# Giving the low halves of the keys all 128 partitions, so that both score products of a decoder's attention contract over 128 rows

## The chip, the cores and the metric

One Trainium2 chip, one core. The metric is the device time of one execution in microseconds (us), as the median of several runs of the whole kernel; the kernel before takes 1324.79 us (three runs, 1317.44 to 1329.73). Engines are called PE (TensorE), DVE (VectorE), ACT (ScalarE), POOL (GpSimd) and SP (SyncE, which issues most transfers); PEld is the weight-load side of PE.

## What is computed

One inference step of a two-layer trunk for a prompt of 1024 tokens and for 8 samples of 4 new tokens each, all in float32. Layer 0 mixes sparse attention with chunked gating, layer 1 is a gated linear recurrence. The change touches the prompt's attention alone: 8 query heads in 2 groups (one per key/value head of 64 features), three branches merged by gates. Cut to what matters:

```python
qg  = q.reshape(B, T, 2, 4, 64)
s_c = einsum('btghd,bngd->bghtn', qg, kc) * scale + bias      # 16 compressed blocks
s_s = einsum('btghd,bgtkcd->bghtkc', qg, k_s) * scale + b_s   # selected blocks
s_w = einsum('btghd,bkgd->bghtk', qg, kw) * scale + bias      # window of 512
p_x = softmax(where(ok, s_x, NEG))
o   = g0 * p_c @ vc + g1 * p_s @ v_s + g2 * p_w @ vw
```

With 1024 tokens there are 16 blocks and 16 are selected, so the selected branch is plain causal attention over all keys so far.

## The kernel before, in words

The program is written engine by engine, with semaphores. Its stages are: normalising and projecting x (0 to about 394 us in the profile), the prompt's attention, the samples' attention, the output projection of layer 0, the recurrent layer, its output projection.

**Two halves for precision.** PE multiplies a reduced float32 (fp32r) at full speed. So operands are split into a high half, the value rounded to fp32r, and a low half, the rest. `q_hl` holds a tile of 128 queries: for the heads of group g the 64 partitions of that group hold the high half and the other 64 partitions hold the low half. `k_hi` holds the high half of the keys of branch b and group g on both halves of the partitions. So one product over 128 rows gives q_hi k_hi + q_lo k_hi. `k_lo` holds the low half of the keys, of group 0 on partitions 0 to 63 and of group 1 on partitions 64 to 127, so a second product over 64 rows adds q_hi k_lo in the same PSUM bank:

```python
mm(o, q_hl[:, i % 2, h, :], k_hi[:, b, g, keys], True, False)
m = mm(o, q_hl[gp, i % 2, h, :], k_lo[gp, b, keys], False, True)
```

These are lines 1353 and 1354; `mm` is a helper, so the profile gives all its products line 1198, and all transposes line 1202. In both, q is the stationary operand (128 columns) and the keys are streamed, up to 512 columns a product. The probabilities are split in the same way for the product with the values, whose two products over 128 rows (lines 1380 and 1381) also accumulate in one bank.

**Order of the attention.** The prompt has 8 tiles i of 128 queries. A tile has one compressed unit ("c") and 16 units of one head each: for each group g, four heads of the selected branch ("s", (i + 1) * 128 key columns) and four of the window ("w", at most 640 columns). A table written by `attention_steps` (lines 130 to 186) gives the order, the same for PE and DVE and nearly the same for ACT. For each block of 128 keys of a group: PE turns four heads' probabilities (4 transposes, line 1368) into one of three PSUM banks; ACT copies their high half into `p_hl` (line 1056) and DVE subtracts for the low half (line 1837); PE multiplies with the values up to two blocks later. In between PE makes the score products of the next group's heads, one unit per block or more, into one of two slots of two banks; DVE adds the bias and takes the minimum (line 1814; the window's farthest block has a table and a minimum of its own, lines 1808 and 1810), and ACT takes the exponential (line 1048). PE's scores of unit n wait until DVE has read unit n - 2. At the end of a tile's group 16 products bring the outputs back (line 1388), and DVE merges them with the gates (lines 1843 to 1856).

**What runs ahead of it.** When the projections end, ACT copies the high halves (lines 1013, 1017, 1020), POOL copies the windowed keys' high half to the other partitions (line 919) and then clears `aS` (line 923), which the recurrent layer needs; POOL's next work is the second norm's scales (line 826). DVE subtracts for `k_lo` (line 1733) and for the values' low half (line 1738), then waits for the bias, which SP loads in 16 transfers after the last projection (line 696). ACT splits the first queries' high half (line 1036) once the semaphore `split_lo` counts 4; DVE makes their low half (line 1770), and PE begins.

The small buffers `region_m` (spatial weights and their bias, later `aS`, `bS` and `small_out`) and `region_g` (the gating norm's scale and shift, later the final norm's) are not in use during the attention.

Of the kernel before, what the change touches and what calls it, by code (L numbers as in the profile page):

```python
# [23 lines left out]
P = 128  # L24
D = 1024
KC = D // P
SEQ = 1024
# [203 lines left out]
def build(nc, ins, outs):  # L231
    ctx = ExitStack()
    with ctx:
        def sb(name, shape):
            return ctx.enter_context(nc.sbuf_tensor(name, shape, F32))
# [11 lines left out]
        def placed(name, at, shape, dt):  # L247

            return nc.alloc_sbuf_tensor_at(name, shape, dt, offset=arena_at + 4 * at)
# [50 lines left out]
        k_hi = placed("k_hi", AT_W + 8448, [P, 2, KVH, SEQ], F32R)  # L300
        k_lo = placed("k_lo", AT_W + 25600, [P, 2, SEQ], F32R)
        v_hl = placed("v_hl", AT_W + 21504, [P, 2, KVH, PT, 2 * HD], F32R)
# [72 lines left out]
        rel_in = sb("rel_in", [BUCKETS + 1, HEADS])  # L375
        vecT = sb("vecT", [P, NVEC])
        region_m = sb("region_m", [P, 1024])
        wspT = view(region_m, 0, 4, P)
# [429 lines left out]
        def _(pool):  # L808
# [112 lines left out]
            pool.wait_ge(k_hi_other, 2)  # L921
            pool.wait_ge(mix_used, TILES)
            pool.memset(aS, 0.0).then_inc(aS_zero, 1)
            for i in range(TILES):
# [16 lines left out]
        def _(act):  # L941
# [82 lines left out]
            for what, n in act_order(steps):  # L1024
                if what == "split_q":
# [3 lines left out]
                    if n == 0:  # L1029
                        act.wait_ge(fm_dve, counts["dve"])  # L1030
                        act.wait_ge(split_hi, 6)
                        act.wait_ge(split_lo, 4)
                        act.wait_ge(vn_out, 16)
# [162 lines left out]
        def _(pe):  # L1196
            def mm(out, l, r, start, stop):
                return nc.tensor.matmul(out, l, r, start=start, stop=stop, skip_group_check=True)  # L1198
# [124 lines left out]

            pe.wait_ge(split_lo, 4)
            pe.wait_ge(split_hi, 6)
# [5 lines left out]
            for what, n in steps:  # L1331
# [3 lines left out]
                if what == "scores":  # L1335
# [5 lines left out]
                    if kind == "c":  # L1341
                        pe.wait_ge(q_lo, i + 1)
                        for c in range(HPG):
                            m = mm(ps[:, slot, c * 2 * NB:(c + 1) * 2 * NB], qT[:, c, tok(i)],
                                   kc_bd[:, :, :].rearrange("p g n -> p (g n)"), True, True)
                    else:
                        g, b = h // HPG, 0 if kind == "s" else 1
                        gp = slice(g * HD, (g + 1) * HD)
                        for a in range(0, cols, 512):
                            w = min(512, cols - a)  # L1350
                            o = ps[:, slot + a // 512, 0:w]
                            keys = slice(first + a, first + a + w)
                            mm(o, q_hl[:, i % 2, h, :], k_hi[:, b, g, keys], True, False)
                            m = mm(o, q_hl[gp, i % 2, h, :], k_lo[gp, b, keys], False, True)
                    m.then_inc(scores_done, 1)
# [197 lines left out]
        def _(dve):  # L1553
# [174 lines left out]
            for b, kT in ((1, kT_w), (0, kT_s)):  # L1728
                v.tensor_copy(k_new[:, b, :], kT[:, SEQ:TOK])
                for g in range(KVH):  # L1730
                    gp = slice(g * HD, (g + 1) * HD)
                    dve.wait_ge(k_hi_own, 2 * (1 - b) + g + 1)
                    v.tensor_tensor(k_lo[gp, b, :], kT[gp, 0:SEQ], k_hi[gp, b, g, :].bitcast(F32), ALU.subtract)
            for b, vv in ((1, v_w), (0, v_s)):
                for g in range(KVH):
# [3 lines left out]
                                    v_hl[:, b, g, :, 0:HD].bitcast(F32), ALU.subtract).then_inc(split_lo, 1)  # L1739
            dve.wait_ge(split_lo, 4)  # L1740
            dve.wait_ge(bias_in[0], 16 * (P // COPIES))
# [383 lines left out]
```

## Time and profile before

| | us |
|---|---|
| median of three runs | 1324.79 |
| the profiled execution | 1331.78 |
| its span, first to last instruction | 1330.0 |
| attention stage, from its first scores to its last value product | 413.8 to 807.5 |
| busy over the span: PE / PEld | 1214.5 / 948.3 |
| busy over the span: DVE / ACT / POOL | 609.0 / 442.9 / 134.2 |
| mean granted clock of PE, share of 2.4 GHz | 0.915 |

A busy PE is one that has a matmul in flight; the ends of matmuls are modelled, so the distance between two starts says more than a duration. The granted clock has two levels, 1.2 and 2.4 GHz, and a value between 0.50 and 1.00 is a mean over a stretch that has both. "issue" as a releaser means that the engine waited for nothing that the profile shows. In a row, "64*128 64x512" is the stationary operand (rows * columns) and the streamed one.

### The profile page before, as it was taken

How to read it: one execution, taken by the hardware profiler on the slowest of the kernel's cores; microseconds unless marked ns; L12 is line 12 of the kernel's file. 1: busy time of each engine (PE TensorE's matmuls, PEld its weight loads, DVE VectorE, ACT ScalarE, POOL GpSimd, SP SyncE). 2: the span in 40 equal slices, each digit the busy share in tenths (PEclk: the TensorE clock that was granted, in tenths of full speed). 3: DMA queues.
4: the chain of work that ended last, by engine and by line, in shares of the span. 5: the costliest groups of instructions: out<-in, count | busy, mean ns of one | idle time of the engine just before them, and what ended most of it. 6: DMA issues, size and time to landing. Idle time of an engine off the chain costs nothing.

```text
span 1330.0 us, 14969 instructions
## 1 busy us (share of the span) xinstructions
PE 1214.5 (91%) x5793; PEld 948.3 (71%) x5793; DVE 609.0 (46%) x1180; ACT 442.9 (33%) x756; POOL 134.2 (10%) x179
## 2 busy tenths in 40 slices
PE   5999999999985988899999997889989999998997
PEld 3555549999983656566666665668868888997884
DVE  1223222121344466674676573354438998324232
ACT  1111122111014445553554451032225777313111
POOL 1222239000010000000000000000011222000110
PEclk9999999999995689896897796579999999998999
DMA  8110102112018000000000006222222111411121
GB/s 292 62 36 17 56 20 66 49 48 45 20 20 108 0 0 1 1 1 1 0 1 1 0 10 200 108 79 95 83 67 81 32 33 33 156 35 48 68 95 55
DMA packets 62372, 70.62 MB, mean 53 GB/s; under 512 B 13529, under 2 KB 47369, under 8 KB 62302
## 3 DMA queue, kind: packets, MB, share of 16 engines
q1 hardware_dynamic: 56924, 64.43, 16.8%
q0 software_dynamic: 2608, 3.59, 0.8%
q10 hardware_dynamic: 2770, 1.65, 0.4%
q8 instruction: 46, 0.75, 0.2%
q14 instruction: 24, 0.20, 0.1%
HBM read 57.47 MB, written 12.17 MB: 52 GB/s over the span
## 4 chain that ended last, share of the span: by engine, by line
PE 83%; ACT 5%; DVE 5%; issue 3%; DMA 3%; SPq 1%; DVEq 0%; POOL 0%; ACTq 0%; POOLq 0%
PE ps L1198 77%; PE ps L1202 6%; ACT region_w L1048 1%; ACT p_hl L1056 1%; DMA region_w<-rel_rows_dram 1%; DVE p_hl L1837 1%; DMA region_y<-in_w_in_a 1%; ACT L1141 1%; ACT region_w L1141 1%; DMA region_w<-in_cache_win 0%; DVE gated L1848 0%; DVE q_hl L1770 0%; SPq L720 0%; SPq L722 0%; DVE region_w L1814 0%
## 5 line engine op out<-in xcount | busy, mean ns | idle before, releaser
L1198 PE MATMUL ps<-h1T_hi,w_c_hl 128*128 128x352 f32 x768 | 151.3, 326 | 12.9 <-ACT region_w L1141 8.7
L1202 PE MATMUL ps<-ident,region_w 128*128 128x128 f32 (+2 forms) x738 | 126.8, 306 | 32.4 <-ACT region_w L1048 15.8
L1202 PEld LDWEIGHTS ps<-ident,region_w 128*128 128x128 f32 (+2 forms) x738 | 103.1, 160 | 66.7 <-DVE p_hl L1837 18.3
L1198 PE MATMUL ps<-hT_hi,w_fm_hl 128*128 128x352 f32 x768 | 146.5, 324 | 2.8 <-DVE w_fm_hl L1654 2.8
L1198 PEld LDWEIGHTS ps<-h1T_hi,w_c_hl 128*128 128x128 f32 x768 | 129.1, 190 | 17.7 <-ACT region_w L1141 13.1
L1837 DVE TENSOR_TENSOR p_hl<-ps,p_hl 128x512 fp32r<-128x512 f32 x132 | 91.2, 691 | 97.2 <-ACT p_hl L1056 96.6
L1198 PEld LDWEIGHTS ps<-hT_hi,w_fm_hl 128*128 128x128 f32 x768 | 127.7, 188 | 3.0 <-DVE w_fm_hl L1654 2.9
L1056 ACT CAST p_hl<-ps 128x512 fp32r<-128x512 f32 x132 | 77.4, 586 | 134.5 <-PE ps L1202 134.3
L1198 PE MATMUL ps<-p_hl,v_hl 128*128 128x512 f32 x264 | 109.9, 501 | 5.4 <-DVE p_hl L1837 3.1
L1198 PE MATMUL ps<-region_y,region_w 128*128 128x512 f32 (+3 forms) x288 | 100.7, 508 | 0.0
L1198 PE MATMUL ps<-region_w 128*128 128x512 f32 (+4 forms) x308 | 98.9, 514 | 1.4 <-DVE region_w L1895 1.4
L1198 PE MATMUL ps<-k_hi,q_hl 128*128 128x512 f32 (+3 forms) x192 | 91.1, 474 | 8.5 <-DVE negm L1814 4.8
L1048 ACT ACTIVATE region_w<-region_w,negm 128x640 f32<-128x640 f32 (+7 forms) x128 | 93.8, 735 | 5.4 <-DVE negm L1814 5.1
L826 POOL TENSOR_SCALAR ms<-ss 128x1 f32<-128x1 f32 (+1 forms) x27 | 12.6, 466 | 794.7 <-ACT region_w L1109 576.7
L1198 PE MATMUL ps<-k_lo,q_hl 64*128 64x512 f32 (+3 forms) x192 | 92.1, 480 | 0.0
L1198 PE MATMUL ps<-w_outa_hi,ya_hl 128*128 128x512 f32 (+1 forms) x288 | 81.4, 401 | 5.2 <-DVE w_outa_lo L1951 5.2
L1198 PE MATMUL ps<-h1T_lo,w_c_hl 128*128 128x352 f32 x384 | 85.9, 325 | 0.0
L1198 PEld LDWEIGHTS ps<-region_y,region_w 128*128 128x128 f32 (+1 forms) x288 | 52.8, 186 | 44.8 <-issue 37.8
L1198 PE MATMUL ps<-hT_lo,w_fm_hl 128*128 128x352 f32 x384 | 82.7, 323 | 0.0
L1198 PEld LDWEIGHTS ps<-region_w 128*128 128x128 f32 (+2 forms) x308 | 47.6, 181 | 43.6 <-issue 32.2
L1814 DVE CUSTOM_DVE_ANT_0 region_w<-ps,region_w 128x128 f32<-128x128 f32 (+7 forms) x96 | 62.7, 664 | 18.4 <-PE ps L1198 17.5
L1198 PEld LDWEIGHTS ps<-k_lo,q_hl 64*128 64x128 f32 x192 | 40.6, 212 | 38.2 <-issue 31.7
(266 smaller groups left out, 1707.9 us busy)
## 6 DMA issues: line engine op xcount, KB each, us to landing
region_w<-in_x_prompt SPq DMA_DIRECT2D x16, 512.0 KB, 3.7
region_w<-in_w_in_c SPq DMA_DIRECT2D x16, 512.0 KB, 4.0
region_w<-in_w_in_a SPq DMA_DIRECT2D x12, 512.0 KB, 3.8
region_w<-rel_rows_dram SPq DMA_DIRECT2D x16, 256.0 KB, 15.8
region_w<-in_cache_nsa SPq DMA_DIRECT2D x16, 256.0 KB, 2.9
region_w<-in_w_out_a SPq DMA_DIRECT2D x2, 2048.0 KB, 12.9
x_dram<-region_w SPq DMA_DIRECT2D x8, 512.0 KB, 2.6
region_w<-in_w_out_c SPq DMA_DIRECT2D x2, 2048.0 KB, 10.0
```

Source lines behind the costliest of these rows:

```text
L826: pool.tensor_scalar(ms[0:r, norm, i:i + 1], ss[0:r, norm, i:i + 1], 1.0 / D, EPS, ALU.mult, ALU.add).then_inc(pool_chain, 1)
L1048: nc.scalar.activation(buf, buf, ACT.Exp, bias=negm[:, n % 16:n % 16 + 1], scale=-1.0, accum_out=sums[:, i % 2, b, h:h + 1]).then_inc(prob ...
L1056: nc.scalar.copy(p_hl[:, f % 2, 0, :], ps[:, 4 + k % 3, :]).then_inc(p_hi, 1)
L1141: nc.scalar.activation(r_buf.rearrange("p (a b) -> p a b", a=3), bank3(n), ACT.Sigmoid, bias=vecT[:, VEC["b_rg_a"] + c:VEC["b_rg_a"] + c + ...
L1198: return nc.tensor.matmul(out, l, r, start=start, stop=stop, skip_group_check=True)
L1202: return nc.tensor.transpose(out, x, ident[0:k, 0:k])
L1814: v.tensor_tensor_reduce(buf[:, 0:cols], src, bias[:, h, SEQ - cols:SEQ], 1.0, 3e38, ALU.add, ALU.min, m).then_inc(logits_ready, 1)
L1837: v.tensor_tensor(p_hl[:, f % 2, 1, :], bank, p_hl[:, f % 2, 0, :].bitcast(F32), ALU.subtract).then_inc(bank_empty, 1)
```

## The change

Group 0 and group 1 get a buffer of their own for the low half of the keys. Both halves of the partitions hold the same low half (DVE makes it twice, the second time writing to the other 64 partitions), and the second score product takes all 128 rows: it now adds q_hi k_lo + q_lo k_lo. The second buffer lies over `region_m` and `region_g`, so POOL's clear of `aS` waits for the last scores. The subtracts count on `split_lo`, so it reaches 6 where it reached 4.

```diff
...
         bias = view(region_w, 0, HEADS, SEQ)
 
         k_hi = placed("k_hi", AT_W + 8448, [P, 2, KVH, SEQ], F32R)
-        k_lo = placed("k_lo", AT_W + 25600, [P, 2, SEQ], F32R)
+        k_lo_0 = placed("k_lo_0", AT_W + 25600, [P, 2, SEQ], F32R)
         v_hl = placed("v_hl", AT_W + 21504, [P, 2, KVH, PT, 2 * HD], F32R)
         q_hl = placed("q_hl", AT_Q + 4 * TOK, [P, 2, HEADS, P], F32R)
         p_hl = placed("p_hl", AT_W + 19200, [P, 2, 2, 512], F32R)
...
         tril_s = sb("tril_s", [NS, NS])
         rel_in = sb("rel_in", [BUCKETS + 1, HEADS])
         vecT = sb("vecT", [P, NVEC])
+        k_lo_1 = nc.alloc_sbuf_tensor_at("k_lo_1", [P, 2, SEQ], F32R, offset=nc.sbuf_base)
+        k_lo = [k_lo_0, k_lo_1]
         region_m = sb("region_m", [P, 1024])
         wspT = view(region_m, 0, 4, P)
         b_sp = view(region_m, 512, 4, P)
...
                                  ).then_inc(k_hi_other, 1)
             pool.wait_ge(k_hi_other, 2)
             pool.wait_ge(mix_used, TILES)
+            pool.wait_ge(scores_done, len(units))
             pool.memset(aS, 0.0).then_inc(aS_zero, 1)
             for i in range(TILES):
                 rms(1, i, TILES + i + 1)
...
                     if n == 0:
                         act.wait_ge(fm_dve, counts["dve"])
                         act.wait_ge(split_hi, 6)
-                        act.wait_ge(split_lo, 4)
+                        act.wait_ge(split_lo, 6)
                         act.wait_ge(vn_out, 16)
                     for g in range(KVH):
                         gp = slice(g * HD, (g + 1) * HD)
...
                        True, True).then_inc(cmp_pe, 1)
 
 
-            pe.wait_ge(split_lo, 4)
+            pe.wait_ge(split_lo, 6)
             pe.wait_ge(split_hi, 6)
             pe.wait_ge(k_hi_other, 2)
             pe.wait_ge(fm_act, counts["act"])
...
                                    kc_bd[:, :, :].rearrange("p g n -> p (g n)"), True, True)
                     else:
                         g, b = h // HPG, 0 if kind == "s" else 1
-                        gp = slice(g * HD, (g + 1) * HD)
                         for a in range(0, cols, 512):
                             w = min(512, cols - a)
                             o = ps[:, slot + a // 512, 0:w]
                             keys = slice(first + a, first + a + w)
                             mm(o, q_hl[:, i % 2, h, :], k_hi[:, b, g, keys], True, False)
-                            m = mm(o, q_hl[gp, i % 2, h, :], k_lo[gp, b, keys], False, True)
+                            m = mm(o, q_hl[:, i % 2, h, :], k_lo[g][:, b, keys], False, True)
                     m.then_inc(scores_done, 1)
                 elif what == "c_turn":
                     pe.wait_ge(probs_ready, 17 * n + 1)
...
                 for g in range(KVH):
                     gp = slice(g * HD, (g + 1) * HD)
                     dve.wait_ge(k_hi_own, 2 * (1 - b) + g + 1)
-                    v.tensor_tensor(k_lo[gp, b, :], kT[gp, 0:SEQ], k_hi[gp, b, g, :].bitcast(F32), ALU.subtract)
+                    for rows_ in (gp, slice((1 - g) * HD, (2 - g) * HD)):
+                        e = v.tensor_tensor(k_lo[g][rows_, b, :], kT[gp, 0:SEQ], k_hi[gp, b, g, :].bitcast(F32),
+                                            ALU.subtract)
+                e.then_inc(split_lo, 1)
             for b, vv in ((1, v_w), (0, v_s)):
                 for g in range(KVH):
                     gp = slice(g * HD, (g + 1) * HD)
                     dve.wait_ge(split_hi, 2 * (1 - b) + g + 1)
                     v.tensor_tensor(v_hl[:, b, g, :, HD:2 * HD], vv[:, 0:PT, gp],
                                     v_hl[:, b, g, :, 0:HD].bitcast(F32), ALU.subtract).then_inc(split_lo, 1)
-            dve.wait_ge(split_lo, 4)
+            dve.wait_ge(split_lo, 6)
             dve.wait_ge(bias_in[0], 16 * (P // COPIES))
             dve.wait_ge(gates_ready, 1)
             dve.wait_ge(vn_out, 16)
```

On DVE, between the last projection and the first tile, these rows stood before (x2 are neighbours that read alike; `k_new` holds the samples' keys):

```order
L1722 TENSOR_SCALAR region_q<-ps 128x1056
L1729 COPY k_new<-region_q 128x32
L1733 TENSOR_TENSOR k_lo<-region_q,k_hi 64x1024 x2
L1729 COPY k_new<-region_q 128x32
L1733 TENSOR_TENSOR k_lo<-region_q,k_hi 64x1024 x2
L1738 TENSOR_TENSOR v_hl<-region_q,v_hl 128x8x64 x4
L1770 TENSOR_TENSOR q_hl<-region_q,q_hl 64x512 x2
```

And these stand there now, where the two buffers of the low half have numbers at their names:

```order
L1724 TENSOR_SCALAR region_q<-ps 128x1056
L1731 COPY k_new<-region_q 128x32
L1736 TENSOR_TENSOR k_lo_57<-region_q,k_hi 64x1024 x2
L1736 TENSOR_TENSOR k_lo_73<-region_q,k_hi 64x1024 x2
L1731 COPY k_new<-region_q 128x32
L1736 TENSOR_TENSOR k_lo_57<-region_q,k_hi 64x1024 x2
L1736 TENSOR_TENSOR k_lo_73<-region_q,k_hi 64x1024 x2
L1743 TENSOR_TENSOR v_hl<-region_q,v_hl 128x8x64 x4
L1775 TENSOR_TENSOR q_hl<-region_q,q_hl 64x512 x2
```

Four subtracts of 64 x 1024 are added, ahead of the values' low half and of the first queries'. On PE the order and the number of the products stay as they were.

## Rows read from the trace of the kernel before

**Rows 1.** Page part 1, busy us of each engine (share of the span) xinstructions

```profile
PE 1214.5 (91%) x5793; PEld 948.3 (71%) x5793; DVE 609.0 (46%) x1180; ACT 442.9 (33%) x756; POOL 134.2 (10%) x179
```

**Rows 2.** Windows: length, busy us of PE, PEld, DVE, ACT, POOL; clock, DMA, GB/s

```profile
413.80:807.50 393.70, 361.71 (x1531) 248.45 (x1532) 244.83 (x642) 195.29 (x441) 0.00 (x0) 0.84 0.06 11
```

**Rows 3.** Chain of waits over 390 to 820 us, shares by engine and line

```profile
by line: PE ps L1198 57.8%; PE ps L1202 13.9%; ACT region_w L1048 4.1%; issue 3.9%; ACT p_hl L1056 3.6%; DMA region_w<-rel_rows_dram 3.5%; DVE p_hl L1837 3.4%; DVE gated L1848 1.1%; DVE q_hl L1770 1.1%; DVE region_w L1814 0.8%; SPq L696 0.7
```

**Rows 4.** Timeline of PE, full clock: start us, us, line, operation, out<-in

```profile
647.10 0.60 PE L1202 MATMUL ps<-ident,region_w 128*128 128x128 f32 x4
647.45 0.48 PE L1198 MATMUL ps<-k_hi,q_hl 128*128 128x512 f32 x1
647.86 0.49 PE L1198 MATMUL ps<-k_lo,q_hl 64*128 64x512 f32 x1
648.28 0.39 PE L1198 MATMUL ps<-k_hi,q_hl 128*128 128x256 f32 x1
...
648.91 0.74 PE L1198 MATMUL ps<-p_hl,v_hl 128*128 128x512 f32 x2
649.48 0.60 PE L1202 MATMUL ps<-ident,region_w 128*128 128x128 f32 x4
...
657.76 0.33 PE L1198 MATMUL ps<-k_hi,q_hl 128*128 128x128 f32 x1
...
658.27 0.73 PE L1198 MATMUL ps<-p_hl,v_hl 128*128 128x512 f32 x2
```

**Rows 5.** Timeline of PE in the output projection

```profile
883.23 1.07 PE L1198 MATMUL ps<-w_outa_hi,ya_hl 128*128 128x512 f32 x4
...
884.59 1.07 PE L1198 MATMUL ps<-w_outa_hi,ya_hl 128*128 128x512 f32 x4
```

**Rows 6.** Timeline of PE's weight loads

```profile
647.86 0.18 PEld L1198 LDWEIGHTS ps<-k_lo,q_hl 64*128 64x128 f32 x1 [0.24 <-issue]
```

**Rows 7.** Page part 5: busy us, mean ns of one, idle before

```profile
L1198 PE MATMUL ps<-k_hi,q_hl 128*128 128x512 f32 (+3 forms) x192 | 91.1, 474 | 8.5 <-DVE negm L1814 4.8
...
L1198 PE MATMUL ps<-k_lo,q_hl 64*128 64x512 f32 (+3 forms) x192 | 92.1, 480 | 0.0
```

**Rows 8.** Timeline of PE at the low clock

```profile
612.31 0.78 PE L1198 MATMUL ps<-k_hi,q_hl 128*128 128x512 f32 x1
613.02 0.79 PE L1198 MATMUL ps<-k_lo,q_hl 64*128 64x512 f32 x1
613.74 0.58 PE L1198 MATMUL ps<-k_hi,q_hl 128*128 128x256 f32 x1
...
614.76 1.22 PE L1198 MATMUL ps<-p_hl,v_hl 128*128 128x512 f32 x2
...
620.66 1.20 PE L1198 MATMUL ps<-p_hl,v_hl 128*128 128x512 f32 x2
```

**Rows 9.** Timeline of DVE in a selected and in a window group

```profile
650.81 0.69 DVE L1837 TENSOR_TENSOR p_hl<-ps,p_hl 128x512 fp32r<-128x512 f32 x1 [0.77 <-ACT p_hl L1056]
651.42 0.95 DVE L1814 CUSTOM_DVE_ANT_0 region_w<-ps,region_w 128x768 f32<-128x768 f32 x1
...
657.89 0.69 DVE L1837 TENSOR_TENSOR p_hl<-ps,p_hl 128x512 fp32r<-128x512 f32 x1 [1.63 <-ACT p_hl L1056]
...
659.51 0.08 DVE L1810 DVE_READ_ACCUMULATOR2_ANT negm<- 128x1 f32 x1
```

**Rows 10.** Timeline ahead of the attention

```profile
399.29 2.45 DVE L1733 TENSOR_TENSOR k_lo<-region_q,k_hi 64x1024 fp32r<-64x1024 f32 x2
...
404.41 1.24 ACT L1036 CAST q_hl<-region_q 64x512 fp32r<-64x512 f32 x2 [1.93 <-DVE v_hl L1738]
...
412.30 1.39 DVE L1770 TENSOR_TENSOR q_hl<-region_q,q_hl 64x512 fp32r<-64x512 f32 x2 [8.06 <-DMA region_w<-rel_rows_dram]
```

**Rows 11.** Windows of 2 us, columns as in rows 2

```profile
602.00:604.00 2.00, 0.88 (x9) 0.66 (x7) 0.94 (x3) 1.22 (x3) 0.00 (x0) 1.00 0.00 0
638.00:640.00 2.00, 2.00 (x8) 1.26 (x6) 1.48 (x4) 0.88 (x2) 0.00 (x0) 0.56 0.00 0
```

## Prediction

> **What bounds the kernel now.** I read the page's busy times first: TensorE (PE) is busy for 91% of the span [rows 1]. That does not yet make it the bound of the stage that is changed, so next come the engines' busy times over the attention stage, from the first compressed scores at 413.8 us to 807.5 us: PE 361.71 us of 393.70, DVE 244.83, ACT 195.29, at a mean granted clock of 0.84, so the stage runs partly at 1.2 and partly at 2.4 GHz [rows 2]. The chain of waits over 390 to 820 us agrees: its largest parts are matmuls of line 1198 with 57.8% and transposes of line 1202 with 13.9% [rows 3]. So this stage follows PE, and PE idles only 32 us in it (393.70 − 361.71).
>
> Then the question is what PE does in a unit. The timeline of PE at full clock, in a selected group of 768 key columns, has one period from 647.10 to 649.48: 2.38 us [rows 4]. Four transposes take 0.35 us of it, the two value products 0.57, and the four score products of one head 1.46, the largest share. A score product of 512 columns starts 0.41 or 0.42 us before the next instruction, of 256 columns (648.91 − 648.28) / 2 = 0.32, and of 128 columns (658.27 − 657.76) / 2 = 0.255. Products on all 128 rows among themselves are much denser: six of 512 columns in the output projection take 884.59 − 883.23 = 1.36 us, 0.23 each [rows 5], although hi and lo parts accumulate there as well; four transposes of 128 columns take 0.35, 0.09 each [rows 4]. So every score product carries about 0.17 to 0.19 us that no other product of its size has. The weight load shows where: the load for the 64-row product begins at 647.86 with its matmul, not ahead of it, after 0.24 us in which the load port waited for nothing the profile names [rows 6]. The same gap stands behind the 64-row product (0.42 us to the next 128-row product, into another bank), so it belongs to the alternation of 64 and 128 rows, once in and once out.
>
> By the Trainium skill, TensorEngine Tiling (Array Packing), Key Properties, a change of tiling mode drains the TensorE. The trace agrees, 0.41 against 0.23 us; by it both gaps go when both products use 128 rows.
>
> **The change part by part.**
> - *Second product on 128 rows.* It removes no product: each 128-row score product stays followed by one with the same columns. By the column counts of the code, the eight prompt tiles have 88 pairs of 512 columns, 24 of 384, 24 of 256 and 56 of 128, together 192, and the page counts 192 of each [rows 7]. For both products of a pair, at full clock: 512: 0.415 − 0.23 = 0.185 each; 128: 0.255 − 0.09 = 0.165. No row shows 256 and 384 columns on 128 rows at full clock; between 0.09 and 0.23 I interpolate 0.13 and 0.18, giving 0.19 each (bounds for these 96 products: 0.09 to 0.23 us each, together 0.19 × 96 = 18 us, at worst 9). Sum: 176 × 0.185 + 96 × 0.19 + 112 × 0.165 = 32.6 + 18.2 + 18.5 = 69 us. At the low clock a 512 product starts 0.71 us before the next and a 256 one 0.51, while two full-row value products behind transposes take 1.20, 0.42 each [rows 8]: 0.29 us instead of 0.185. With a third of the 384 products at the low clock and up to 0.1 us more for each, that adds some 10. PE thus sheds about 79 us.
> - *What of it the span sees.* PE is not alone for long. In the 768-column period DVE needs 0.61 us to the end of its low half of the probabilities (650.81 to 651.42), 0.95 for the minimum and 0.08 for its read: about 1.6 us [rows 9]. PE would need 2.38 − 4 × 0.19 = 1.62. So such a unit falls from 2.38 to about 1.65 and gives 0.73 of 0.76. A window unit of 640 columns has two minima: 657.89 to 659.51 plus 0.08, 1.70 us [rows 9]. PE's unit is 0.35 + 0.57 + 2 × 0.415 + 2 × 0.255 = 2.26 and would be 1.56; DVE's 1.70 decides, so 0.56 of 0.70 comes through. For tiles 4 to 7, 32 units of each kind: 32 × 0.73 + 32 × 0.56 = 41 us. If the low level's share of the stage, worked out below as a third, holds there too, some 20 of these units run at it; PE stays the bound in them, four gaps give 2 × 0.29 + 2 × 0.24 = 1.06 us, some 0.4 more than at full clock: 8. Tiles 0 to 3 hold 64 units with one pair each; 16 × (0.33 + 0.38 + 0.38 + 0.37) = 23 us of PE, and some 3 more with a third at the low clock. Of these 26 I take three quarters, 20, since short units wait for DVE in turn. Together 69. At each of the 31 changes of group DVE comes with a backlog that it did not have; I take 0.2 us each, 6 off: 63.
> - *Four more subtracts on DVE before the stage.* Two take 2.45 us [rows 10], so four cost 4.9. They end the lows of v near 404.3 + 4.9 = 409.2 instead of 404.3; ACT's copy of q waits for that and then takes 1.24, done at 410.6. The cover is the load of the bias: DVE waits 8.06 us for it until 412.30 [rows 10], so 1.7 us of cover remain and I cost the subtracts at 0. Writing the other 64 partitions is what the low of q does too: 1.39 us for two of 512 columns [rows 10], no dearer per column. If the cover were gone, the cost would be at most 4.9.
> - *POOL's clear of its 128 × 320 buffer now waits for the last score.* Queued behind it are POOL's scales of the second norm, for rows that the output projection makes; that projection is under way at 883 us [rows 5], and the last score comes before 807.5 [rows 2]. ACT asks for the cleared buffer later still. Cost 0. The counts that ACT and PE wait for rise from 4 to 6 and end with the subtracts above.
> - *The clock.* In 602 to 604 us PE was busy for 0.88 of 2.00 us at 1.00; the low level followed, and the mean of 638 to 640 is still 0.56 [rows 11]. Denser products could end such stretches sooner, longer waits for DVE could start more of them. The mean of 0.84 means 0.16 × 2 × 394 = 126 us at the low level [rows 2]. I give it a gain of 2, with 0 to +25 as the good side and a rival for the bad one.
>
> Sum: 65 us off the profiled execution of 1331.78 us: 1267. That execution lies 7 us above the median of 1324.79, so against the median: 1260.
>
> **The rivals.**
> - *DVE and ACT take the place.* All engines of a unit work in a ring: ACT copies the high half, DVE waits for it, PE waits for both. If only a third of the 79 us comes through, 26 us, 1299. For it: DVE's sum is 244.83 us, and 1.6 against 1.62 us leaves no slack in a unit. Against: two thirds of DVE's time in the window is enough now.
> - *The clock comes back with the density.* If half of the 126 us at the low level vanish, 63 us, each worth 1 − 2.38 / 4.18 = 0.43 us [rows 4, 8], some 25 more come off: 1235. For it: a low-clock stretch with fewer gaps is worked off sooner. Against: no row shows what the denser products do to the clock.
> - *Nothing changes.* The page's mean duration of a product is the same for both: 480 ns for 64 rows, 474 for 128 [rows 7]. If the gaps come from accumulating twice into one bank, they stay: 1325. Against it stand two value products in one bank that start 0.42 us apart at the low clock, where score products take 0.71 [rows 8], and the gap towards another bank. The Trainium skill's TensorE: Matmul & The Clock Gate, Why this matters for your kernels, gives a product on 32 rows the same time as one on 128; by that alone the change is worth 0. The trace's durations agree with it, its start times do not.
> - *Slower: the stage stays at the low clock.* Waiting for DVE, PE pauses more often, the clock falls and does not return. From the first to the last of rows 8 lie two low-clock units, 8.35 us, 4.18 each; without its four gaps it would be 3.1, against 2.38 now at full clock. Now the stage's work is 267 us at full clock and 126 us at the low one, worth 126 × 2.38 / 4.18 = 72, together 339; at 3.1 / 2.38 = 1.30 it would take 441, 47 us more: 1372. At full clock it takes 0.70 of that work, so this decides once some three quarters of the work runs at the low level.
>
> **How the numbers follow.** My forecast 0.62 (1260, by itself 1240 to 1282), DVE and ACT 0.15, better clock 0.12, nothing 0.07, slower 0.04. About 1%, 13 us, is what a measurement can tell here. Faster by over 1%: 0.62 + 0.15 + 0.12 = 0.89; within 1%: 0.07; slower: 0.04. The range 1220 to 1298 takes in all but the last two cases and a part of the DVE case: the low end is all 79 us of PE and the clock's 25, the high end a third of the gain.
>
> **What would show it.** Right: score products of 512 columns start 0.22 to 0.25 us apart at full clock with their loads ahead of them; PE's busy time falls by some 60 to 80 us; DVE's wait for ACT's high half shrinks in the full-clock units; the first scores still start near 413.8. Wrong: gaps of 0.4 us that remain, or a stage that ends no earlier with PE's idle time grown by as much as its work shrank, or a mean granted clock below 0.6 in the stage.

## The result, and the profile after

The changed kernel takes 1257.60 us as the median of four runs (1254.07 to 1259.37), the kernel before 1327.26 us in the runs beside it (four, 1317.44 to 1336.00): a ratio of 0.947, 95% interval 0.940 to 0.955, so 70 us faster. The profiled execution took 1259.37 us, its span is 1257.5 us.

The page's busy times, to be read against [rows 1]:

```profile
PE 1122.7 (89%) x5793; PEld 919.8 (73%) x5793; DVE 608.3 (48%) x1184; ACT 444.4 (35%) x756; POOL 134.4 (11%) x179
```

PE lost 92 us of busy time with as many instructions as before; DVE has four more and the same time. The windows of the changed kernel (columns as in [rows 2]): the whole attention stage, then the tiles 3, 5 and 7 of it, each from its compressed scores to those of the next (tile 7 to its last value product):

```profile
415.30:735.60 320.30, 271.68 (x1531) 220.78 (x1532) 239.31 (x642) 196.81 (x441) 0.37 (x1) 0.91 0.08 14
501.44:537.82 36.38, 28.95 (x172) 22.60 (x170) 28.74 (x72) 23.23 (x54) 0.00 (x0) 1.00 0.00 0
580.46:626.81 46.35, 42.03 (x245) 34.48 (x244) 36.65 (x92) 30.60 (x61) 0.00 (x0) 0.93 0.00 1
677.32:735.60 58.28, 50.45 (x296) 39.77 (x295) 44.19 (x99) 36.90 (x69) 0.37 (x1) 1.00 0.16 47
```

and the same three tiles of the kernel before:

```profile
511.17:551.15 39.98, 34.14 (x171) 22.47 (x170) 28.81 (x72) 23.23 (x54) 0.00 (x0) 1.00 0.00 0
603.84:670.51 66.67, 63.83 (x245) 43.36 (x244) 37.92 (x92) 30.21 (x61) 0.00 (x0) 0.74 0.00 1
734.01:807.70 73.69, 67.52 (x296) 45.35 (x295) 46.11 (x100) 36.37 (x69) 0.00 (x0) 0.91 0.12 37
```

The stage went from 393.70 us [rows 2] to 320.30: 73.4 us, the whole gain. Two things are in it. Tile 3 ran at the full granted clock in both kernels and gave 3.6 us for 16 units, which is what the gaps alone are worth there. Tile 5 gave 20.3 us, and its clock rose from 0.74 to 0.93 as well. To part the two, take the time at the low level as (1 − mean clock) × 2 × length, and 0.43 us lost in each such microsecond, the prediction's figure from [rows 4, 8]:

| stage of | length | clock | at the low level | lost to it | the rest |
|---|---|---|---|---|---|
| before | 393.7 | 0.84 | 126 | 54 | 340 |
| after | 320.3 | 0.91 | 58 | 25 | 295 |

So about 45 us come from the work itself and 29 from the clock. This is an estimate: the clock is printed to a hundredth, which leaves ±2 us on each "rest", and the 0.43 is from one kind of unit of the kernel before, of 768 columns, at the two levels. All runs on record can be set beside it, since each has a span and a mean granted clock. With (1 − clock) × 2 × span as a run's time at the low level, a straight line through 29 runs of the kernel before (its longest ones left out) rises by 0.36 us for each such microsecond, one through ten of the changed kernel by 0.30. Their mean times at the low level are 212 and 146 us, so the clock's part is rather 20 to 24 us, and the work's 47 to 51 of the 71 between the mean spans. The 45 and 29 used below are the estimate from the two profiles.

TensorE's timeline in a window unit of 640 columns and in a selected one of 768, to be read against [rows 4]:

```profile
594.97 0.47 PE L1201 MATMUL ps<-k_hi,q_hl 128*128 128x512 f32 x1
595.28 0.39 PE L1201 MATMUL ps<-k_lo,q_hl 128*128 128x512 f32 x1
595.51 0.22 PE L1201 MATMUL ps<-k_hi,q_hl 128*128 128x128 f32 x1
595.57 0.28 PE L1201 MATMUL ps<-k_lo,q_hl 128*128 128x128 f32 x1
595.68 0.68 PE L1201 MATMUL ps<-p_hl,v_hl 128*128 128x512 f32 x2
596.19 0.60 PE L1205 MATMUL ps<-ident,region_w 128*128 128x128 f32 x4
596.55 0.48 PE L1201 MATMUL ps<-k_hi,q_hl 128*128 128x512 f32 x1
...
606.26 0.48 PE L1201 MATMUL ps<-k_hi,q_hl 128*128 128x512 f32 x1
606.58 0.40 PE L1201 MATMUL ps<-k_lo,q_hl 128*128 128x512 f32 x1
606.81 0.28 PE L1201 MATMUL ps<-k_hi,q_hl 128*128 128x256 f32 x1
606.93 0.28 PE L1201 MATMUL ps<-k_lo,q_hl 128*128 128x256 f32 x1
607.05 0.63 PE L1201 MATMUL ps<-p_hl,v_hl 128*128 128x512 f32 x2
...
607.88 0.48 PE L1201 MATMUL ps<-k_hi,q_hl 128*128 128x512 f32 x1
```

The periods are 1.58 us (596.55 − 594.97) and 1.62 us (607.88 − 606.26), against 2.26 and 2.38 before. Starts are 0.23 us apart after a second product of 512 columns, 0.12 for 256, 0.06 to 0.11 for 128. Only the first of a unit still keeps 0.31. It is not the bank: a unit of 1024 columns in tile 7 has a second pair of 512 into one bank, 0.24 us apart:

```profile
704.44 0.40 PE L1201 MATMUL ps<-k_hi,q_hl 128*128 128x512 f32 x1
704.68 0.40 PE L1201 MATMUL ps<-k_lo,q_hl 128*128 128x512 f32 x1
```

By the weight loads of the window unit's next period the low product's load stands behind the high product's, which follows the transposes' loads:

```profile
596.52 0.19 PEld L1201 LDWEIGHTS ps<-k_hi,q_hl 128*128 128x128 f32 x1
596.63 0.19 PEld L1201 LDWEIGHTS ps<-k_lo,q_hl 128*128 128x128 f32 x1
596.87 0.19 PEld L1201 LDWEIGHTS ps<-k_hi,q_hl 128*128 128x128 f32 x1
```

The load ends at 596.82 and its matmul starts at 596.86. That the load holds this matmul back fits these times, but no run tested it. VectorE's timeline ahead of the stage, and in the window unit above:

```profile
397.04 5.66 DVE L1736 TENSOR_TENSOR k_lo<-region_q,k_hi 64x1024 fp32r<-64x1024 f32 x4
...
402.82 4.91 DVE L1736 TENSOR_TENSOR k_lo<-region_q,k_hi 64x1024 fp32r<-64x1024 f32 x4
407.77 2.50 DVE L1743 TENSOR_TENSOR v_hl<-region_q,v_hl 128x512 fp32r<-128x512 f32 x4
413.76 1.39 DVE L1775 TENSOR_TENSOR q_hl<-region_q,q_hl 64x512 fp32r<-64x512 f32 x2 [3.50 <-DMA region_w<-rel_rows_dram]
...
596.00 0.69 DVE L1842 TENSOR_TENSOR p_hl<-ps,p_hl 128x512 fp32r<-128x512 f32 x1
...
597.61 0.08 DVE L1815 DVE_READ_ACCUMULATOR2_ANT negm<- 128x1 f32 x1
597.61 0.69 DVE L1842 TENSOR_TENSOR p_hl<-ps,p_hl 128x512 fp32r<-128x512 f32 x1
```

Of the 8.06 us of waiting for the bias [rows 10] 3.50 are left: the four subtracts were covered. The path by way of ACT is tighter: its copy of the first queries (410.43, 1.24 us) ends 2.1 us before DVE starts at 413.76. In the unit DVE needs 1.61 us (597.61 − 596.00; the next low half starts with the read of the minimum, not behind it) and PE 1.58, so neither waits much. Over the stage DVE's group of the low half of the probabilities, before and then after, shows where its slack went (busy, mean ns | idle before, releaser):

```profile
L1837 DVE TENSOR_TENSOR p_hl<-ps,p_hl 128x512 fp32r<-128x512 f32 x132 | 91.2, 691 | 97.2 <-ACT p_hl L1056 96.6
```

```profile
L1842 DVE TENSOR_TENSOR p_hl<-ps,p_hl 128x512 fp32r<-128x512 f32 x132 | 91.0, 690 | 58.5 <-ACT p_hl L1059 57.4
```

POOL's timeline shows the new wait; POOL, which ran the clear right behind its copies before, does nothing else in that time, and no instruction waits for it:

```profile
721.67 0.37 POOL L926 MEMSET region_m<- 128x320 f32 x1 [322.51 <-PE ps L1201]
```

### The profile page after: what moved, and what is told of

Same layout as the page of the kernel before. It is cut to its first block, busy times and chain, and to the rows that moved or that the text cites. A ratio compares the mean times of both kernels' runs of the same rounds, so it can differ in the third digit from the quotient of the medians.

```text
span 1257.5 us, 14973 instructions
## 1 busy us (share of the span) xinstructions
PE 1122.7 (89%) x5793; PEld 919.8 (73%) x5793; DVE 608.3 (48%) x1184; ACT 444.4 (35%) x756; POOL 134.4 (11%) x179
## 3 DMA queue, kind: packets, MB, share of 16 engines
q10 hardware_dynamic: 2770, 1.65, 0.5%
## 4 chain that ended last, share of the span: by engine, by line
PE 72%; DVE 11%; issue 7%; ACT 6%; DMA 3%; SPq 1%; DVEq 0%; POOL 0%; ACTq 0%; POOLq 0%
PE ps L1201 68%; PE ps L1205 4%; DVE region_w L1819 2%; DVE p_hl L1842 2%; ACT p_hl L1059 2%; DVE region_w L1815 2%; ACT region_w L1051 1%; DMA region_w<-rel_rows_dram 1%; DMA region_y<-in_w_in_a 1%; ACT L1144 1%; ACT region_w L1144 1%; DVE gated L1853 1%; DVE region_w L1813 1%; DVE q_hl L1775 0%; DMA region_w<-in_cache_win 0%
## 5 line engine op out<-in xcount | busy, mean ns | idle before, releaser
L1205 PE MATMUL ps<-ident,region_w 128*128 128x128 f32 (+2 forms) x738 | 120.8, 296 | 38.2 <-ACT region_w L1051 20.2
L1205 PEld LDWEIGHTS ps<-ident,region_w 128*128 128x128 f32 (+2 forms) x738 | 98.2, 154 | 71.0 <-DVE p_hl L1842 21.3
L1842 DVE TENSOR_TENSOR p_hl<-ps,p_hl 128x512 fp32r<-128x512 f32 x132 | 91.0, 690 | 58.5 <-ACT p_hl L1059 57.4
L1201 PE MATMUL ps<-p_hl,v_hl 128*128 128x512 f32 x264 | 98.3, 455 | 9.0 <-DVE p_hl L1842 7.5
L1201 PE MATMUL ps<-k_hi,q_hl 128*128 128x512 f32 (+3 forms) x192 | 77.8, 406 | 16.7 <-DVE negm L1819 11.4
L1201 PEld LDWEIGHTS ps<-h1T_lo,w_c_hl 128*128 128x128 f32 x384 | 66.1, 189 | 0.0
L1201 PEld LDWEIGHTS ps<-w_outa_hi,ya_hl 128*128 128x128 f32 (+1 forms) x288 | 52.2, 183 | 19.1 <-issue 5.4
L1201 PEld LDWEIGHTS ps<-hT_lo,w_fm_hl 128*128 128x128 f32 x384 | 65.6, 189 | 0.0
```

The lines of the kernel that those rows point to most:

```text
L1205: return nc.tensor.transpose(out, x, ident[0:k, 0:k])
L1842: v.tensor_tensor(p_hl[:, f % 2, 1, :], bank, p_hl[:, f % 2, 0, :].bitcast(F32), ALU.subtract).then_inc(bank_empty, 1)
```

## The experiments

Ten kernels ran. The first three ask where the gain comes from, the others what bounds the stage now. "Ratio" is to the kernel before in the same batch, with its 95% interval; "low" and "rest" are worked out for each run's profiled stage as in the table above.

| run | median us | ratio | stage us | clock | low us | rest us |
|---|---|---|---|---|---|---|
| e1_rows64 | 1327.49 | 0.997 (0.992 to 1.002) | 393.2 | 0.83 | 134 | 336 |
| e2_group0 | 1282.46 | 0.967 (0.962 to 0.972) | 342.1 | 0.92 | 55 | 319 |
| e3_order | 1294.26 | 0.972 (0.966 to 0.979) | 362.0 | 0.86 | 101 | 318 |
| e4_no_low | 1257.36 | 0.948 (0.943 to 0.953) | 314.1 | 0.90 | 63 | 287 |
| e5_warm | 1253.31 | 0.948 (0.944 to 0.952) | 315.2 | 0.94 | 38 | 299 |
| e6_short_low | 1221.58 | 0.924 (0.918 to 0.930) | 286.4 | 0.91 | 52 | 264 |
| e7_dve_only | 1231.48 | 0.929 (0.924 to 0.934) | 292.4 | 0.95 | 29 | 280 |
| e8_pool | 1247.97 | 0.941 (0.937 to 0.945) | 306.8 | 0.95 | 31 | 294 |
| e9_after_again | 1254.61 | 0.945 (0.941 to 0.949) | 315.9 | 0.93 | 44 | 297 |
| e10_both | 1247.08 | 0.940 (0.936 to 0.945) | 308.5 | 0.94 | 37 | 293 |

**e1_rows64**: the changed kernel with its second product on 64 rows again; the buffers, the subtracts and POOL's wait stay.

```diff
+                        gp = slice(g * HD, (g + 1) * HD)
...
-                            m = mm(o, q_hl[:, i % 2, h, :], k_lo[g][:, b, keys], False, True)
+                            m = mm(o, q_hl[gp, i % 2, h, :], k_lo[g][gp, b, keys], False, True)
```

> The changed kernel with the second score product back on the group's own 64 rows; both buffers, the four more subtracts and the later clear on POOL stay. Theory (the gaps come from the alternation of 128 and 64 rows, all else is covered): the gaps return, score products of 512 columns start 0.41 us apart at full clock, and the time is that of the kernel before, ratio 0.995 to 1.01. Rival (part of the gain comes from the buffers, or the subtracts cost something that the gain hid): clearly under 0.985, or over 1.01.

Measured: the kernel before, in time and in its stage. Products of 512 columns start 0.40 and 0.43 us before the next again (651.62, 652.02, 652.45). The subtracts and POOL's wait cost nothing that shows, and the buffers alone give nothing: the gain belongs to the 128 rows.

**e2_group0**: 128 rows for group 0 only, half of the 384 gaps gone.

```diff
+                        gp = slice(0, P) if g == 0 else slice(HD, P)
...
-                            m = mm(o, q_hl[:, i % 2, h, :], k_lo[g][:, b, keys], False, True)
+                            m = mm(o, q_hl[gp, i % 2, h, :], k_lo[g][gp, b, keys], False, True)
```

> The changed kernel with 128 rows in the second product for the heads of group 0 alone, 64 rows for group 1. Theory: half of the 384 gaps go, so about half of the gain of 70 us: 1285 to 1300 us, and within one run group 0's products of 512 columns start 0.23 to 0.27 us apart and group 1's 0.41. Rival (the gain is above all the clock's, which comes back only when everything is dense): under a quarter of the gain, over 1310, with a mean granted clock in the stage near 0.84.

Measured: 45 of the 70 us (1327.56 less 1282.46), a little more than expected. TensorE's timeline of this run, a unit of group 0 and then one of group 1:

```profile
600.01 0.47 PE L1201 MATMUL ps<-k_hi,q_hl 128*128 128x512 f32 x1
600.32 0.39 PE L1201 MATMUL ps<-k_lo,q_hl 128*128 128x512 f32 x1
600.55 0.28 PE L1201 MATMUL ps<-k_hi,q_hl 128*128 128x256 f32 x1
...
618.60 0.48 PE L1201 MATMUL ps<-k_hi,q_hl 128*128 128x512 f32 x1
619.01 0.50 PE L1201 MATMUL ps<-k_lo,q_hl 64*128 64x512 f32 x1
619.44 0.38 PE L1201 MATMUL ps<-k_hi,q_hl 128*128 128x256 f32 x1
```

In one program the starts are 0.31 and 0.23 us apart in group 0, 0.41 and 0.43 in group 1. By the estimate the rest of the stage fell by 21 us (340 to 319), half of the 45, while the time at the low level fell to 55 us, as far as with the whole change. So the clock's part came with half of the gaps already, and the gaps' part went by their number.

**e3_order**: the kernel before, in which a unit with two pieces issues both 128-row products, then both 64-row ones: two changes of shape in the place of four, the same products.

```diff
                             mm(o, q_hl[:, i % 2, h, :], k_hi[:, b, g, keys], True, False)
+                        for a in range(0, cols, 512):
+                            w = min(512, cols - a)
+                            o = ps[:, slot + a // 512, 0:w]
+                            keys = slice(first + a, first + a + w)
                             m = mm(o, q_hl[gp, i % 2, h, :], k_lo[gp, b, keys], False, True)
```

> The kernel before, still with 64 rows in the second product, but in units of two pieces both 128-row products come first and both 64-row products after them. Theory (each change between 64 and 128 rows costs 0.17 to 0.19 us): the 64 units of tiles 4 to 7 have two changes instead of four, 128 gaps go, 128 x 0.18 = 23 us of PE, of which the span sees 15 to 25: 1300 to 1312. Rival (a 64-row product is slow as such, or the gap comes from accumulating into a bank): no gap goes, within 1% of the kernel before.

Measured: 33 us off (the 1327.56 us of its batch less 1294.26), more than the 15 to 25 expected. By the estimate 22 of it are work (340 to 318, half of the 45 for a third of the gaps, all of them in long units), as the theory had it, and 11 the clock, which it had left out. TensorE's timeline of this run, a window unit of 640 columns:

```profile
665.77 0.60 PE L1202 MATMUL ps<-ident,region_w 128*128 128x128 f32 x4
666.12 0.54 PE L1198 MATMUL ps<-k_hi,q_hl 128*128 128x512 f32 x2
666.59 0.55 PE L1198 MATMUL ps<-k_lo,q_hl 64*128 64x512 f32 x2
667.08 1.10 PE L1198 MATMUL ps<-two_i,part_sb 128*128 128x64 f32 x8
```

The two products on 128 rows take 0.47 us with the change behind them, the two on 64 rows 0.49 with theirs; with a change behind every product the kernel before needed 2 × 0.415 + 2 × 0.255 = 1.34 us for the four, here 0.96. So 64 rows are no slower as such, and it is the change that costs. PE's busy time fell by 35 us (361.71 [rows 2] to 326.55); less 0.43 for each of the 25 us at the low level that went, 24 us remain for 128 changes (64 units, two each): 0.19 each, the size that the prediction gave them. The rival of the banks is not settled by this run, because the two products into one bank no longer stand side by side in it. The changed kernel settles it: there they still do, and the second pair of a 1024-column unit starts 0.24 us apart.

**e4_no_low**: the changed kernel without the second score product.

```diff
-                            mm(o, q_hl[:, i % 2, h, :], k_hi[:, b, g, keys], True, False)
-                            m = mm(o, q_hl[:, i % 2, h, :], k_lo[g][:, b, keys], False, True)
+                            m = mm(o, q_hl[:, i % 2, h, :], k_hi[:, b, g, keys], True, True)
```

> The changed kernel without the second score product; the scores lack the part with the keys' low half. PE sheds 192 more products, some 0.2 us each, 35 to 40 us. Theory (since the change DVE and ACT take as long as PE in a unit: 1.6 us against 1.62 in a group of 768 columns): the span falls by less than 15 us, over 1243. Rival (PE still sets the pace of the stage): 25 to 40 us less, under 1233.

Measured: no change in time (1257.36). PE's busy time in the stage fell by another 24 us, to 247.45:

```profile
414.50:728.60 314.10, 247.45 (x1339) 190.81 (x1340) 236.89 (x642) 196.17 (x441) 0.37 (x1) 0.90 0.08 16
```

The rest went down by some 8 us in this execution, the fastest of the five (1250.36 us, mean clock 0.939 over its span). The other four ran at 0.929 to 0.932, the ten of the changed kernel at 0.938 to 0.946, so there the clock took that gain back. PE alone no longer sets the pace.

**e5_warm**: the changed kernel with 20 products put into PE's wait ahead of the first scores.

```diff
...
+            for _ in range(20):
+                mm(ps[:, 7, :], ident[:, :], yT[:, 4, 0:512], True, True)
             pe.wait_ge(split_lo, 6)
...
```

(Three of PE's other waits, cut here, moved ahead of the products.)

> The changed kernel with 20 added products of 128x512 (their results are not used) put on TensorE into the about 20 us in which it waits for the bias rows ahead of the first scores. Theory: the low granted clock from about 415 to 441 us and in the stretches after it follows that wait; with the wait filled, the first tile starts at the high level, most of the 58 us of low-clock time that are left go, and the kernel takes about 1248 us (8 to 10 less than the changed kernel, so under both kernels). Rival: the first tiles are bound by the round trips between TensorE, VectorE and ScalarE and by the bias load, so the clock there decides nothing and the time is within 3 us of the changed kernel; or the added products raise the power drawn and the low stretches come at another place, with the same sum.

Measured: 1253.31 us in six runs (1250.98 to 1257.66), against 1254.61 for the changed kernel in a later batch, 1257.60 in the first: nothing that can be told from zero. The windows of this run show why:

```profile
395.00:413.90 18.90, 17.40 (x40) 7.52 (x40) 15.25 (x16) 9.68 (x12) 2.79 (x2) 1.00 1.08 135
...
415.00:417.00 2.00, 1.34 (x8) 0.93 (x7) 1.32 (x10) 1.15 (x6) 0.00 (x0) 1.00 1.09 130
417.00:419.00 2.00, 1.08 (x7) 1.07 (x6) 0.30 (x2) 0.88 (x5) 0.00 (x0) 0.64 1.09 130
419.00:421.00 2.00, 1.07 (x6) 0.88 (x5) 1.11 (x5) 1.88 (x4) 0.00 (x0) 0.50 1.07 127
```

The wait was filled and the clock stayed up through it, but PE then pauses between the first tile's short units (1.34 and 1.08 us of work in 2 us), and the clock falls 4 us into the stage. The expectation was wrong in the place: it is not only that wait which lets the clock fall.

**e6_short_low** and **e7_dve_only**: both cut DVE's low half of the probabilities to 8 columns; e6 also drops the second value product, e7 keeps it, on the high half.

```diff
-                    v.tensor_tensor(p_hl[:, f % 2, 1, :], bank, p_hl[:, f % 2, 0, :].bitcast(F32),
+                    v.tensor_tensor(p_hl[:, f % 2, 1, 0:8], bank[:, 0:8], p_hl[:, f % 2, 0, 0:8].bitcast(F32),
...
-                    mm(o, v, p_hl[:, f % 2, 1, :], False, b == cols // P - 1).then_inc(values_done, 1)
+                    mm(o, v, p_hl[:, f % 2, 0, :], False, b == cols // P - 1).then_inc(values_done, 1)
```

(The second pair of lines is e7's.) e6 leaves the low half of the probabilities out of the result, e7 counts the high half twice in its place.

> The changed kernel without the second value product, and with VectorE's low half of the probabilities cut to 8 columns: the low half of the probabilities is left out of the result. Theory: after the change the unit is a tie of TensorE (1.6 us), VectorE (1.6) and ScalarE (three operations, about 1.6 to 1.7 with their issue); VectorE sheds some 66 us and TensorE 30 to 60 in the stage, but ScalarE keeps the period near 1.6, so the kernel gains under 20 us (about 1240 to 1255). Rival: VectorE alone sets the pace after the change; then the period falls towards 1.2 and the kernel gains 35 us or more (under 1222).

> The changed kernel with VectorE's low half of the probabilities cut to 8 columns and the second value product fed with the high half again: VectorE sheds some 65 us in the stage, TensorE and ScalarE keep all their instructions; the low half of the probabilities is left out of the result. Theory now: after the change VectorE's chain sets the pace of a unit, so most of the 36 us that the short low half together with one value product less gave comes here too, about 1222 to 1235. Rival: there TensorE and VectorE had to be relieved together; then with TensorE as it is the gain is under 12 us, 1246 or more.

Measured: 1221.58 and 1231.48. My theory for e6, that ScalarE would keep the unit at 1.6 us, fell: 36 us came off the changed kernel of the first batch, 33 off the later one. In e7 DVE alone was relieved and gave 23 us (1254.61 − 1231.48), in e4 PE alone gave none. The stage of e7:

```profile
415.40:707.80 292.40, 256.73 (x1531) 211.54 (x1532) 178.12 (x642) 194.21 (x441) 0.36 (x1) 0.95 0.08 14
```

DVE did 61 us less, and 17 of it came through in the rest of the stage, some 6 more by the clock. That is no more for each microsecond relieved than in e4, where of PE's 24 us some 8 came through. So neither engine is a bound by itself, and DVE has more to relieve. With DVE relieved PE still counts: from e7 to e6 the rest falls by another 16 us by the estimate. The medians differ by 10, but they are of two batches, and the intervals of their ratios overlap.

**e8_pool**, **e9_after_again**, **e10_both**: two jobs of DVE go to POOL, the low halves of the queries and the adds of the gated sums, with POOL's waits for its own earlier instruction; e9 is the changed kernel again, as their measure; e10 has e5's products too.

```diff
             pool.wait_ge(mix_used, TILES)
+            for what, n in steps:
+                if what == "split_q":
...
+                        e = pool.tensor_tensor(q_hl[other, n % 2, hs, :], qT[gp, :, tok(n)],
+                                               q_hl[gp, n % 2, hs, :].bitcast(F32), ALU.subtract)
...
+                    pool.tensor_tensor(a, gated[:, 0], ac, ALU.add).then_inc(acc_half, 1)
+                    pool.wait_ge(acc_half, 2 * i + g + 1)
+                    pool.tensor_tensor(a, gated[:, 1], a, ALU.add).then_inc(acc_ready, 1)
...
             pool.wait_ge(scores_done, len(units))
...
```

> The changed kernel with two jobs of VectorE that touch only SBUF moved to GpSimd, which is idle in the stage: the low halves of the queries (16 instructions of 0.69 us) and the two adds of the gated sums (30 of 0.43 us), some 24 us less on VectorE, the same result. Theory (VectorE sets the pace): about half of it reaches the end, as 62 us shed gave 34 to 36: 10 us less than the changed kernel, about 1247. Rival: these jobs lie where VectorE has slack, or GpSimd's slower instructions hold up the next tile's first scores, and the time is within 4 us of the changed kernel or above it.

> The changed kernel itself, on the chip on which the others of this batch run, as the measure for them: about 1257 us.

> The two edits together that keep the result, the jobs on GpSimd and the 20 added products in TensorE's wait ahead of the first scores. If each gains by itself, 4 us from the filled wait and 10 from GpSimd, about 1243; if neither does, the changed kernel's 1257.

Measured: e8 takes 1247.97 us (six runs, 1244.95 to 1251.75), e9 1254.61 (six, 1250.28 to 1257.19), e10 1247.08. POOL's groups in e8's stage:

```profile
L939 POOL TENSOR_TENSOR q_hl<-region_q,q_hl 64x512 fp32r<-64x512 f32 x16 | 20.4, 1278 | 37.7 <-ACT q_hl L1072 37.0
L954 POOL TENSOR_TENSOR acc<-gated,region_q 128x256 f32<-128x256 f32 x16 | 11.8, 737 | 245.9 <-DVE gated L1878 245.9
L956 POOL TENSOR_TENSOR acc<-gated,acc 128x256 f32<-128x256 f32 x16 | 11.7, 728 | 1.3
```

POOL takes 1278 ns where DVE takes 686 and 737 where DVE takes 425, but nothing else runs on it. The median is 6.6 us better and the computation is the whole one, so this version leads both kernels; the intervals of e8's and e9's ratios overlap, so its lead over the changed kernel is likely rather than settled. By the estimate only 3 of the 9 us by which its stage is shorter are work, the others clock. e5's products add nothing that shows here either.

## Why the prediction was right, and where its terms were not

The time (1260) and the sign came out; two of the terms in the sum were wrong, in opposite directions.

- *The cause, a gap at each change between 64 and 128 rows: right.* e2 shows the gap in one group and not in the other, e3 removes two of four without touching the rows of any product, e1 brings all of them back. The Trainium skill, TensorEngine Tiling (Array Packing), Key Properties, has a change of mode drain the TensorE; the runs agree in that a change costs time, 0.19 us for each one that e3 saved, and do not show what the engine does in it. The rule behind the rival "nothing changes" (the Trainium skill's TensorE: Matmul & The Clock Gate, Why this matters for your kernels: few rows take the time of all) agrees too, with e3's 0.47 against 0.49 us, but only for products of one shape in a row; between shapes it says nothing of the drain.
- *PE sheds 69 us at full clock: mis-sized by the first product of a unit.* It took 0.23 us for each 512-column product; the first one keeps 0.31. 80 units begin with 512 columns, 80 × 0.08 is some 6 us, so 63, and units that begin with fewer columns keep a little too. The trace says 61: 361.71 − 271.68 = 90 of busy time, less 0.43 × 68 us that left the low level.
- *The two units: right in size.* 768 columns were put at 1.65 us and take 1.62. For 640 columns I let DVE decide with 1.70, which adds 0.08 for the read of the minimum; the next instruction starts with that read (both at 597.61), so DVE's period is 1.61 and PE's 1.58 fits it.
- *What the span sees, 63 us: too much.* Some 10 of the 63 were what the gaps cost more at the low level (8 in the long units, 2 in the short ones), which the table above books to the clock; against the other 53 the estimate has 45. PE's idle time in the stage grew from 32 to 48.6 us (320.30 − 271.68), and that is the difference between its 61 and the stage's 45. The step that failed here is the three quarters taken of tiles 0 to 3: with the same estimate tile by tile they gave 9 us where 17 were put down, tiles 4 to 7 34 of 41 (before the 6 for the changes of group). Tiles 0, 1 and 2 took 20.1, 36.0 and 41.3 us at mean clocks of 0.50, 0.65 and 0.83 before, 17.0, 32.3 and 36.9 at 0.50, 0.66 and 0.91 after. Tile 3, at full clock in both kernels, gave 3.6 us of the 5.9 (16 × 0.37) that its gaps are worth, and PE idles 7.4 us in it where it idled 5.8. In tile 7 the idle time grew too, from 6.2 to 7.8 us, so the long units also passed on a little less than the 0.73 and 0.56 us that were put down.
- *The clock, "a gain of 2": the term that failed.* The time at the low level fell from 126 to 58 us, which is worth 29 by the estimate and 20 to 24 by the runs. Beside the 2, some 10 of the 63 were of this kind, so 12 us were put down for it. I had priced this as a rival (25 us for half of the 126) and given it 0.12, because no row showed what denser products do. It came true together with a smaller gain from the gaps, so what happened is a mixture of the two. In the prediction's terms 53 + 12 = 65 stands against 45 + 29 = 74 (72 between the profiled executions). That the two lie so near is luck: the errors have opposite signs.
- *DVE and ACT take the place: half true.* They do so after most of the gain, not after a third. DVE's wait for ACT's high half shrank from 96.6 to 57.4 us, and by e4 and e7 PE and DVE now bound the stage jointly.
- *Slower by the clock: no.* The mean clock rose to 0.91. PE does pause more, and where it pauses most (tiles 0 and 1) the clock still falls.
- *Subtracts, POOL's wait: 0, right* (2.1 us of cover left where 1.7 were forecast; e1). "No dearer per column" was misread, 1.36 against 1.20 ns in [rows 10], but two subtracts to the own partitions and two to the others took 4.91 us, twice the 2.45. The first scores start at 415.30 in the place of 413.80, in e1 at 418.70, each time behind the bias, for which DVE still waits 3.50 and 4.43 us; the total of e1 is that of the kernel before.

## What to carry to other kernels

Where products on few rows alternate with products on all of them, look at start-to-start times, not at durations: each change of shape cost 0.19 us here at the full clock, and the mean durations (474 and 480 ns [rows 7]) hid it. A second copy that fills the rows (or zeros, which were not tried), or merely grouping products of a shape, take it away, the copy at the price of a buffer and a few instructions elsewhere. And a busy engine's saving should be followed into the next engine of the ring and into the granted clock, each with its own term.

## What was not expected of the hardware

The low clock level can outlast a pause by far. Windows of the kernel before, in tile 5, the same pause as in [rows 11]:

```profile
604.00:606.00 2.00, 2.00 (x12) 1.29 (x11) 1.22 (x4) 0.58 (x1) 0.00 (x0) 0.90 0.00 0
...
612.00:620.00 8.00, 8.00 (x21) 4.75 (x20) 3.31 (x6) 3.02 (x6) 0.00 (x0) 0.50 0.00 0
...
630.00:640.00 10.00, 10.00 (x35) 7.58 (x34) 4.65 (x15) 2.29 (x5) 0.00 (x0) 0.51 0.00 0
```

Tile 5 spends some 35 us at the low level ((1 − 0.74) × 2 × 66.67), in most of which PE's records leave no idle time. e2, after an alike pause at the same place of the program, keeps the full clock:

```profile
594.00:596.00 2.00, 0.89 (x8) 0.61 (x6) 1.00 (x3) 1.28 (x3) 0.00 (x0) 1.00 0.00 0
596.00:598.00 2.00, 2.00 (x16) 1.78 (x15) 1.19 (x4) 0.59 (x1) 0.00 (x0) 1.00 0.00 0
```

and e3, which still has two changes a unit, loses tile 5's stretch but spends 34 us at the low level in tile 6 (its mean clock there is 0.74), most of it from 685 us to the tile's end. The runs of one program differ as well: the changed kernel had 58 us at the low level in its first profile and 44 in e9. The low-clock time thus went down with the number of gaps (none in tiles 4 and 7 after, 6.5 us in tile 5), but whether the gaps themselves, the shape of the products or the place of a pause decides it was not taken apart, and stays open.
